# The order of eleven products in each pair of a Strassen-Winograd projection, and the steps between them

## The reference

```python
z = rms_norm(h) @ w_in                       # 1024 x 3584
cb, cc, ch = split(z[..., :1536], 3)         # convolution branch, 4 tiles of 128 columns each
y_conv = group_rms_norm(cb * causal_dwconv3(cc * ch, conv_w), 8 groups)
rq, rk, rv, rg = split(z[..., 1536:], 4)     # retention branch, 4 heads of 128
o = chunkwise_retention(rotary(rq), rotary(rk), rv)
y_ret = group_rms_norm(o, 4 groups) * silu(rg)
h = h + concat([y_conv, y_ret]) @ w_out
```

## Time and profile before

| | |
|---|---|
| time, median of 3 runs | 2276.51 us (2276.47 to 2277.23) |
| the profiled execution's own time | 2279.18 us |
| its span in the profile | 2277.4 us |
| TensorE clock granted, mean | 0.997 of full |
| the stage of the 11 pairs | from 1287.9 to 1552.1 us |
| starts of P1, pairs 0, 1, 5, 8, 10 | 1287.88, 1314.29, 1421.24, 1485.29, 1530.68 us |
| PE idle before an instruction, 1280 to 1560 us | 3.7 us in all |

### The profile page before, as it was taken

How to read it: one execution, slowest core, us unless ns; L and a number is a source line. 1 busy time by engine, 2 the same in 40 slices (tenths; PEclk the granted TensorE clock), 3 DMA queues, 4 the chain that set the end, 5 groups by cost and what they waited for, 6 DMA issues and landing times.

```text
span 2277.4 us, 32520 instructions
## 1 busy us (share of the span) xinstructions
PE 2258.3 (99%) x10806; PEld 1890.5 (83%) x10806; DVE 1635.3 (72%) x2305; ACT 899.5 (39%) x1467; POOL 1199.4 (53%) x1357
## 2 busy tenths in 40 slices
PE   9999999999999999999999999999999999999998
PEld 7888888888888888888888888888888888888887
DVE  7666666756778778876666877666787787787766
ACT  5233333324645434443432224322453444344433
POOL 4332323234566566656546665664556665666562
PEclk9999999999999999999999999999999999999999
DMA  4111010124264555455213111112335645554553
GB/s 157 37 29 37 29 37 28 38 74 148 93 209 149 178 184 202 144 188 185 111 56 120 65 38 38 56 56 85 134 133 185 202 145 187 184 194 144 196 194 139
DMA packets 59722, 273.82 MB, mean 120 GB/s; under 512 B 7152, under 2 KB 10352, under 8 KB 41712
## 3 DMA queue, kind: packets, MB, share of 16 engines
q1 hardware_dynamic: 59056, 270.51, 34.5%
q10 hardware_dynamic: 576, 2.13, 0.2%
HBM read 210.75 MB, written 61.87 MB: 120 GB/s over the span
## 4 chain that ended last, share of the span: by engine, by line
PE 92%; DVE 4%; DVEq 2%; ACT 1%; issue 0%; DMA 0%; POOL 0%; SPq 0%; ACTq 0%
PE prod_ps L959 9%; PE prod_ps L961 9%; PE prod_ps L960 9%; PE prod_ps L1225 8%; PE prod_ps L1227 8%; PE prod_ps L1226 8%; PE side_ps L1225 7%; PE side_ps L1226 7%; PE side_ps L1227 7%; PE side_ps L1100 2%; PE side_ps L1012 2%; PE prod_ps L1648 1%; PE prod_ps L1650 1%; PE prod_ps L1649 1%; PE prod_ps L1636 1%; PE prod_ps L1637 1%
## 5 line engine op out<-in xcount | busy, mean ns | idle before, releaser
L959 PE MATMUL prod_ps<-operand_hi,w_hi 128*128 128x512 f32 x984 | 392.9, 399 | 2.5 <-DVE operand_lo L1825 2.1
L961 PE MATMUL prod_ps<-operand_hi,w_lo 128*128 128x512 f32 x984 | 385.1, 391 | 0.0
L960 PE MATMUL prod_ps<-operand_lo,w_hi 128*128 128x512 f32 x984 | 384.4, 391 | 0.0
L710 POOL CAST w_hi<-w_raw 128x1024 fp32r<-128x1024 f32 x59 | 64.2, 1089 | 470.1 <-PE prod_ps L961 412.3
L755 POOL TENSOR_TENSOR w_lo<-w_raw,w_hi 128x256 fp32r<-128x256 f32 x168 | 155.5, 945 | 129.4 <-ACT w_hi L3027 128.7
L714 POOL TENSOR_TENSOR w_lo<-w_raw,w_hi 128x256 fp32r<-128x256 f32 x236 | 217.2, 951 | 4.7
L959 PEld LDWEIGHTS prod_ps<-operand_hi,w_hi 128*128 128x128 f32 x984 | 185.5, 188 | 39.1 <-DVE operand_lo L1825 2.6
L961 PEld LDWEIGHTS prod_ps<-operand_hi,w_lo 128*128 128x128 f32 x984 | 185.1, 188 | 39.5
L960 PEld LDWEIGHTS prod_ps<-operand_lo,w_hi 128*128 128x128 f32 x984 | 185.4, 188 | 35.7
L755 POOL TENSOR_TENSOR w_lo<-w_s,w_hi 128x256 fp32r<-128x256 f32 x168 | 129.2, 772 | 141.7 <-ACT w_more_hi L3035 114.6
L2236 DVE TENSOR_TENSOR x_res<-prod_ps,x_res 128x512 f32<-128x512 f32 x130 | 89.1, 685 | 95.7 <-PE prod_ps L1227 95.7
(11 more groups left out here) (450 smaller groups left out, 6376.8 us busy)
## 6 DMA issues: line engine op xcount, KB each, us to landing
w_raw<-stream SPq DMA_DIRECT2D x202, 512.0 KB, 3.7
x_park<-x_res SPq DMA_DIRECT2D x45, 1024.0 KB, 8.2
x_res<-x_park SPq DMA_DIRECT2D x45, 1024.0 KB, 6.7
swapped<-op_park SPq DMA_DIRECT2D x39, 1024.0 KB, 5.1
op_park<-swapped SPq DMA_DIRECT2D x6, 1024.0 KB, 7.8
x_in<-x_t SPq DMA_DIRECT2D x16, 256.0 KB, 5.4
x_res<-x_t SPq DMA_DIRECT2D x8, 512.0 KB, 4.5
end_park<-x_res SPq DMA_DIRECT2D x4, 1024.0 KB, 3.8
```

Of the source, the lines that this page charges most:

```text
L959: nc.tensor.matmul(into, w_h, a_h, start=(k == 0), stop=False)
L960: nc.tensor.matmul(into, w_h, a_l, start=False, stop=False)
L961: last = nc.tensor.matmul(into, w_l, a_h, start=False, stop=(k == KT - 1))
```

## The change

In PE's list each pair's order is changed from

P1, P5, P2, c11, P6, c12, P3, P7, c22, P4, c21 (in the last pair P7 ahead of P3, and P4 ahead of c22) to

P1, P5, P2, P6, P3, P7, c11, P4, c12, c22, c21 in all pairs. P3 is now the first in b_z and c12 is added to it. The steps go behind other products. POOL makes S2's, S3's, S4's and A22's low parts ahead of those of the upper tiles, and begins a pair behind P6 of the pair before as it did, though P6 now comes sooner. ACT's copies `copy_u2` and `copy_u3` stand ahead of what stood between them, and some of its other work is moved. In DVE's list only heads 2 and 3 are moved a little. Counts of `in_prod` that others wait for are renumbered.

```diff
@@ gpsimd, split_paired
-                    behind(4)
+                    behind(3)
...
-                behind(5)
-                if not j:
-                    pool.wait_ge(prod, 2 * u)
-                pool.wait_ge(w_landed[1], u * 8 + 16)
-                upper(0).then_inc(in_parts, 1)
-                behind(6)
+                behind(4)
...
                 low(in_a22_lo[:], raw[:, 6:8], in_more_hi[:, 4:6], 4).then_inc(w_split, 1)
+                behind(6)
+                if not j:
+                    pool.wait_ge(prod, 2 * u)
+                pool.wait_ge(w_landed[1], u * 8 + 16)
+                upper(0).then_inc(in_parts, 1)
@@ tensor, paired (new text)
                 then("P2")
+                copied(1)
                 part(4)
                 sum_ready(2)
                 seventh(b_u, S2, T2, False).then_inc(in_prod, 1)
+                part(5)
                 free(n_z)
+                seventh(b_z, S4, B22, True)
+                then("P3")
                 copied(3)
                 sum_ready(3)
                 seventh(b_u, S3, T3, False).then_inc(in_prod, 1)
                 then("P7")
+                part(6)
+                plain(b_w, 0, 0, False).then_inc(in_prod, 1)
+                then("c11")
+                pe.wait_ge(w_split, u + 1)
                 copied(4)
                 sum_ready(4)
                 seventh(b_u, A22, T4, False).then_inc(prod, 2)
                 then("P4")
+                plain(b_z, 0, 1, False).then_inc(in_prod, 1)
+                then("c12")
+                pe.wait_ge(w_split, u + 2)
+                plain(b_v, 1, 1, False).then_inc(in_prod, 1)
+                then("c22")
                 plain(b_u, 1, 0, False).then_inc(prod, 2)
@@ the steps
-            paired(0, {"P2": old(1, "v"), "c11": old(1, "kv"), "P7": old(1, "o")})
+            paired(0, {"P2": old(1, "v"), "P7": old(1, "kv"), "c12": old(1, "o")})
-            paired(2, {"P2": old(2, "kv"), "c12": old(2, "o"), "P4": new(3, "scores")})
-            paired(3, {"P2": old(2, "back"), "c11": new(3, "k"), "c12": old(3, "v"), "c22": old(3, "kv")})
+            paired(2, {"P2": old(2, "kv"), "P4": old(2, "o"), "c21": new(3, "scores")})
+            paired(3, {"P3": old(2, "back"), "c11": new(3, "k"), "P4": old(3, "v"), "c12": old(3, "kv")})
-            conv_after[1]["P4"], ...   conv_after[3]["P6"], ...   conv_after[4]["P4"], ...
+            conv_after[1]["c21"], ...  conv_after[3]["P7"], ...   conv_after[4]["c21"], ...
@@ vector
             out_done(1)
             dve.drain()
-            make_qx(2)
             k_half(2, 1)
-            norm_factor(2 + HEADS1)
             k_half(2, 0)
             qk_made()
+            norm_factor(2 + HEADS1)
+            make_qx(2)
             normed(2 + HEADS1 + 3)
...
@@ scalar, pairs 0 and 1
             copy_p5(0)
             take_ret_v(1)
+            copy_u2(0)
             in_high_more(0)
+            copy_u3(0)
             act.wait_ge(end1_parked[0], 16)
             in_t_high_of(T4, 4)
             in_high_raw(1)
-            copy_u2(0)
             in_high_s12(1)
-            copy_u3(0)
+            in_high_more(1)
             take_ret_o(1)
-            in_high_more(1)
             ret_root(1)
 
             copy_p1(1)
@@ scalar, pair 4
-            copy_p5(4)
-            take_ret_o(3)
-            sigmoid(2, 0)
             copy_u2(4)
             in_high_raw(5)
+            take_ret_o(3)
+            copy_u3(4)
+            high(1, 0)
+            in_high_s12(5)
+            sigmoid(2, 0)
+            in_high_more(5)
             high(2, 0)
             ret_root(3)
-            in_high_s12(5)
             sigmoid(2, 1)
-            copy_u3(4)
@@ scalar, conv_pair
+                copy_u2(j)
                 in_high_raw(j + 1)
+                copy_u3(j)
+                if behind_copies is not None:
+                    behind_copies()
                 in_high_s12(j + 1)
                 in_high_more(j + 1)
...
-            conv_pair(3, behind_p1=lambda: conv_squares(1), behind_u2=lambda: conv_root(1), last=lambda: conv_high(1))
+            conv_pair(2, last=(lambda: conv_high(0), lambda: conv_squares(1)))
+            conv_pair(3, behind_copies=lambda: conv_root(1), last=(lambda: conv_high(1),))
```

More of the change, by code:

```diff
@@ L1666, in paired @@
                 then("P2")
+                copied(1)
                 part(4)
[L1668 to L1671, removed]
                 sum_ready(2)
                 seventh(b_u, S2, T2, False).then_inc(in_prod, 1)
-                then("P6")
+                part(5)
                 free(n_z)
[L1676 to L1689, removed]
+                seventh(b_z, S4, B22, True)
+                then("P3")
                 copied(3)
@@ L1733, in _ @@
             conv_after = [{} for _ in range(3 * CONV_TILES // 2)]
-            conv_after[1]["P4"], conv_after[2]["c11"] = lambda: conv_sums(0), lambda: conv_spread(0)
-            conv_after[3]["P6"], conv_after[3]["c22"] = lambda: conv_sums(1), lambda: conv_spread(1)
-            conv_after[4]["P4"], conv_after[5]["c11"] = lambda: conv_sums(2), lambda: conv_spread(2)
+            conv_after[1]["c21"], conv_after[2]["c11"] = lambda: conv_sums(0), lambda: conv_spread(0)
+            conv_after[3]["P7"], conv_after[3]["c22"] = lambda: conv_sums(1), lambda: conv_spread(1)
+            conv_after[4]["c21"], conv_after[5]["c11"] = lambda: conv_sums(2), lambda: conv_spread(2)
             for n, after in enumerate(conv_after):
@@ L2607, in _ @@
             k_half(3, 0)
+            out_done(2)
+            make_qx(3)
             k_half(3, 1)
             qk_made()
-            out_done(2)
-            make_qx(3)
+            norm_factor(3 + HEADS1)
             v_half(3, 1)
-            take_scores(3)
-            norm_factor(3 + HEADS1)
             v_half(3, 0)
@@ L3451, in _ @@
             copy_p5(1)
+            copy_u2(1)
             in_high_raw(2)
-            copy_u2(1)
+            copy_u3(1)
             in_high_s12(2)
-            copy_u3(1)
+            in_high_more(2)
             take_ret_back(1)
-            in_high_more(2)
             take_ret_v(2)
@@ L3461, in _ @@
             copy_p5(2)
+            copy_u2(2)
             in_high_raw(3)
-            copy_u2(2)
+            copy_u3(2)
             in_high_s12(3)
-            copy_u3(2)
+            in_high_more(3)
             take_ret_o(2)
-            in_high_more(3)
             ret_root(2)
@@ L3471, in _ @@
             copy_p5(3)
+            copy_u2(3)
+            in_high_raw(4)
             take_ret_back(2)
+            copy_u3(3)
+            in_high_s12(4)
             sigmoid(0, 0)
-            in_high_raw(4)
-            copy_u2(3)
+            in_high_more(4)
+            take_ret_v(3)
             high(0, 0)
-            in_high_s12(4)
             sigmoid(0, 1)
-            take_ret_v(3)
-            copy_u3(3)
             high(0, 1)
-            in_high_more(4)
             sigmoid(1, 1)
             high(1, 1)
+            copy_p1(4)
             sigmoid(1, 0)
-            copy_p1(4)
-            high(1, 0)
             copy_p5(4)
-            take_ret_o(3)
-            sigmoid(2, 0)
             copy_u2(4)
             in_high_raw(5)
+            take_ret_o(3)
[4 more added lines that the diff above has]
+            in_high_more(5)
             high(2, 0)
             ret_root(3)
-            in_high_s12(5)
             sigmoid(2, 1)
-            copy_u3(4)
             high(2, 1)
-            in_high_more(5)
             sigmoid(3, 1)
@@ L3523, in conv_pair @@
                     copy_p1(j)
-                if behind_p1 is not None:
-                    behind_p1()
                 copy_p5(j)
+                copy_u2(j)
                 in_high_raw(j + 1)
-                copy_u2(j)
-                if behind_u2 is not None:
-                    behind_u2()
+                copy_u3(j)
+                if behind_copies is not None:
+                    behind_copies()
                 in_high_s12(j + 1)
-                copy_u3(j)
-                if behind_u3 is not None:
-                    behind_u3()
                 in_high_more(j + 1)
-                if last is not None:
-                    last()
+                for step in last or ():
+                    step()
             conv_pair(0)
-            conv_pair(1, behind_u3=lambda: conv_squares(0), last=lambda: conv_root(0))
-            conv_pair(2, behind_u2=lambda: conv_high(0))
-            conv_pair(3, behind_p1=lambda: conv_squares(1), behind_u2=lambda: conv_root(1), last=lambda: conv_high(1))
-            conv_pair(4, behind_u3=lambda: conv_squares(2), last=lambda: conv_root(2))
-            conv_pair(5, behind_u2=lambda: conv_high(2))
+            conv_pair(1, last=(lambda: conv_squares(0), lambda: conv_root(0)))
+            conv_pair(2, last=(lambda: conv_high(0), lambda: conv_squares(1)))
+            conv_pair(3, behind_copies=lambda: conv_root(1), last=(lambda: conv_high(1),))
```

(2 more changed lines are left out.)

18 lines of the change are left out of this document (6 added, 12 removed).

## The result

The changed kernel takes 2315.67 us (median of 4 runs, 2313.16 to 2317.86) against 2276.61 for the kernel before on the same chip: a ratio of 1.0164, 95% interval [1.0152, 1.0177]. It is slower by 1.6%, more than the forecast of 2309.0 and within its range. The profiled execution took 2315.88 with a span of 2314.1, against 2277.4 before: 36.7 us more. PE's busy time, which stood at 2258.3, is

What follows compares the result with a forecast made beforehand. PE, busy 99% of the span, was taken to bound the kernel. Terms for waits and clock falls summed to 32.5 us on the profiled 2279.18, giving 2311.7, less 2.7 to the median: 2309.0 us, range 2295 to 2321.

Steps and rivals of the forecast that it cites:

- P3 of pair 0: Product P3 waits for S4's low part, as ACT's high part stands behind `copy_u2(0)`: 2.9 us, at least 2.7.
- P4 of pair 0: Product P4 waits for T4's low part, behind DVE's unbroken work that starts at c11: 9.7 us, lower end 7.9.
- Scores(2): In pair 1 the old 1.83 us wait goes with its clock tail, having 15 us more: -3.4 us.
- Pairs 2 to 4: Scores(3), o(3) and `copy_p1(4)` late, 0.9 us together (0 to 2); `copy_u3(4)` now ahead of the root, -1.5.
- back(3): End of pair 4: waits for DVE's normed, 2.0 us, taken as 1.6 because POOL is off at the end.
- Pair 5: ACT's copies come late behind normed and the gates, so P7 and partly P2 and P6 wait: 5.6 us.
- Pair 8: DVE's chain from c11 of pair 7 delays the square ahead of `copy_p1(8)`; P6 and partly P2 wait: 6.9 us.
- Behind pair 10: Convolution sums after the last pair wait 0.8 us (0 to 2.0); the old 0.4 us wait ahead goes.
- The clock: PE's clock falls behind four of five waits longer than 1.83 us, 1.6 each: 6.4 us (1.6 to 12.8).
- only the heads' start pays: Rival, 17%: pairs 0 and 1 stall, later chains shrink and are hidden: +13.5 us, 2290.
- Everything is late: Rival, 15%: bank releases covered by 0.5 us come late too, each wait has a clock tail: 2321 to 2329 us.
- Faster: Rival, 4%: T4's low part ready within 0.25 us of c11's end, the two old waits go: -5.3 us, 2271.2.

Runs made afterwards that it cites:

- the lists mended: Changed kernel with the other engines' lists fitted wherever PE waited: 2278.68 us; also the kernel before with its two waits mended by lists: 2275.32 us.
- tile 1 in pair 8: Changed kernel with DVE's bank reads ahead of an odd tile's taps, and tile 1's squares, sums and spread later in pair 8: 2307.84 us.
- the squares of tile 1 behind: Changed kernel with only conv_squares(1) moved in ACT's list, from ahead of copy_p1(8) to behind copy_u2(8): 2312.18 us.

## Why the prediction was right, and where it was off

The mechanism was right: PE's work is the same, the covers went, several chains of DVE and ACT are late, and the two old waits are gone. The sum of 32.5 was against 36.7 in the profile. (The terms' low ends as written add to +20.7 and their high ends to +45.0, where the prediction has +18 and +44.) Term by term, predicted and measured:

- **P3 of pair 0**, 2.9: 2.69. The row of POOL's low part and the copy ahead of it behave as in the earlier trace rows.
- **P4 of pair 0**, 9.7: 9.25. DVE's chain took 8.99 for 9.46; the rotary pieces are 1.12 beside POOL, as in the earlier trace rows, and T4's own part fell to 1.23 from 1.78 when POOL was done. The Trainium skill (GPSIMD Engine Reference, Specifications) has POOL share its SBUF interfaces with VectorE; the two prices agree.
- **P6 of pair 1**, 3.0: 2.65. **Scores(2)**, -3.4: as forecast between the two traces. In the medians less than this was to be had: 25 of the 39 runs of the kernel before timed beside the experiments show a mean clock of 0.999. That leaves at most 3.4 us lost in the whole run, and the low stretch that stands at the end of every trace (from 2272.1 us here, behind the last matmul) takes 2.6 of them; with a tail of 1.7 the mean would be 0.998. So most runs had no tail behind scores(2), and the profiled one had that and another fall near its start.
- **Pairs 2 to 4**, 0.9 - 1.5: the total is near, the place not. None of scores(3), o(3) and `copy_p1(4)` waited; v(3) did, for 0.99, as `take_k(3)` stands behind a gate in DVE's list. I had not followed that item.
- **back(3)**, 1.6: 3.04. I took DVE's chain off with a discount for an idle POOL, and POOL was busier than before: 10.2 of the chain's 12.4 us where it had been 6.6 of 11.3. DVE itself was busy for 10.5 in place of 9.4; it had not started late (c11's add at 1425.42 had waited 0.85 for PE). The row gave 2.0 without the discount; a busier POOL fits the other 1.0, but no run took POOL's work away to show it.
- **Pair 5**, 5.6: 3.95 (0.77 + 3.18). **Pair 8**, 6.9: 4.99 (3.22 + 1.77). DVE's chain of pair 7 took 19.3 us (1500.21 to 1519.50) where it was 20.5; c22's bank made the larger part of the wait, P6's copy the rest. In both pairs I had stayed too high by more than a quarter, the other way than at back(3).
- **Behind pair 10**, 0.8 - 0.4: 0.64 (sums of tile 3) and 0.4 gone. The sums of tile 2, at the end of pair 9, which I had called covered, waited 0.25.
- **The clock**, 6.4: 12.7. This is the term that was mis-sized most: "longer than the one of 1.83 us, after which the clock fell", four times 1.6. Seven stretches had a fall, three of them outside my list: back(3), and the two sums steps, ahead of which PE waited 0.25 and 0.64 only. In pair 8 it came behind P2 and not behind P6. The one behind P4 cost 2.8. And P3, on my list with 2.69 us, had none. A threshold on the wait ahead is the wrong rule. That the time fell within the range owes something to luck: a clock term of half the true size met terms for pairs 5 and 8 that were 3.6 too high.

Of the rivals, "only the heads' start pays" fell: pairs 4, 5 and 8 hold 12.0 us of waits. "Everything is late" fell too: of the bank releases one was late (c22's at P2 of pair 8), and the waits of 0.77, 0.99 and 1.77 had no tail. "Faster" asked for T4 within 0.25 us of c11's end; it came 9.25 late. The forecast of the median, 2309.0, missed 2315.67 by 6.7: 4.2 in the sum, the rest because I carried the profile's 2.7 above the median over, while the profiled run of the changed kernel lay at its median. The 2.7 were in good part two falls of the clock, the one behind scores(2) and one near the start, that most executions lack.

## What to carry over

When an order of matmuls on a full engine is changed, list for each product the last item that it needs on every other engine and how far down its list that item stands. Free work that nothing holds back (T4, a high part) belongs ahead of work that waits for the new late product, and a copy that PE asks for belongs ahead of a root that waits for DVE. Mend the places in one kernel and read the waits again: a single repair pushes part of its gain to the next item of the same list. And count PE's clock with each new wait: 11.0 of the 37.3 us were clock. Compare single executions by their waits, since falls of the clock come and go between them.

## What the hardware did that was not expected

- In the changed kernel the clock did not fall after a wait of 2.69 us (P3, window 1.00), nor after 1.77; with the lists mended not after 1.02 or 1.51. It fell after 1.83, 2.65, 3.04, 3.18, 3.22 and 9.25. So the order of lengths does not settle it. Nor does the place: P3 of pair 0 waits for 2.69 us in seven of the traces, with the clock at 1.00 behind it in six. In the seventh (tile 1 in pair 8, an edit far behind this point) it is 0.50 from 1296.2 to 1303.0 us:

```profile
1296.80:1300.00 3.20, 3.17 (x8) 2.49 (x9) 0.00 (x0) 0.00 (x0) 3.12 (x5) 0.50 0.46 116
```

  The Trainium skill (TensorE: Matmul & The Clock Gate, What's actually happening) says that the gate goes by how busy PE has been recently, which is wider than one wait; the rows don't contradict that, and don't show what it counts.
- It fell with hardly a wait: behind the convolution's sums of tile 2 (16 matmuls of two columns, 0.25 us idle ahead of them) the matmuls of 512 columns from 1564.04 on start 0.42 apart:

```profile
1561.49 1.92 PE L1038 MATMUL side_ps<-ones,o_sq 128*128 128x2 f32 x16 [0.25 <-ACT o_sq L2855]
...
1564.04 0.62 PE L1636 MATMUL prod_ps<-operand_hi,w_hi 128*128 128x512 f32 x1
1564.46 0.63 PE L1637 MATMUL prod_ps<-operand_lo,w_hi 128*128 128x512 f32 x1
```

  In the kernel with the squares of tile 1 behind, the same step with the same 0.25 us ahead of it had a clock of 1.00 behind it (from 1561.3 to 1566.0 us). Whether a fall comes is thus not fixed by the step.
- The runs of a kernel with many waits lie further apart: 2304.57 to 2314.04 us with pair 8 mended, at mean clocks of 0.995 and 0.991, against 2276.01 to 2279.22 for the kernel before at 0.997 to 0.999. Falls that come in some executions and not in others, as the two places above show, would make this; that was not traced run by run.
